# Moving the tensors of a two-block transformer kernel to other byte positions in SBUF

## The reference

```python
def first_block(...):                     # 2 layers; 512 latent + 256 context tokens
    for l in range(2):
        h = modulate(rms_norm(x, norm1_g[l]), sh1, sc1)
        qa, ka, va, qb, kb, vb, ga, gb = split_in_proj(h @ w_in[l])
        ya = window_attention_latent(...); yb = full_attention_latent(...)
        x = x + gt1 * ((sigmoid(ga) * (ya @ w_pa) + sigmoid(gb) * (yb @ w_pb)) @ w_o)
        h2 = modulate(rms_norm(x, norm2_g[l]), sh2, sc2)
        x = x + gt2 * ((silu(h2 @ w_gate) * (h2 @ w_up)) @ w_down)
        # in layer 0 the same is done for the context tokens
    return rms_norm(x, final_norm_g)

def second_block(x, ...):                 # 1 layer
    proj = rms_norm_2(x, norm_gain) @ w_in
    y_a = (nsa_mixer(...) * silu(g_nsa)) @ w_proj_a      # compressed, selected and windowed attention
    y_b = (rglru_mixer(u_lru, ...) * silu(g_lru)) @ w_proj_b
    return x + (sigmoid(gate_a) * y_a + sigmoid(gate_b) * y_b) @ w_out
```

## Time and profile before

| what | value |
|---|---|
| median of 3 runs | 2462.16 us |
| span of the profiled execution | 2459.3 us |
| mean granted TensorE clock | 0.992 of full |
| TensorE matmul busy | 2379.4 us, 97% |
| VectorE busy | 1547.7 us, 63% |
| ScalarE busy | 1129.1 us, 46% |
| chain that ended last | 79% TensorE |
| DMA, mean | 109 GB/s |

### The profile page before, as it was taken

The page is one execution under the profiler, slowest core; times in us unless marked ns, Lnnn a source line. Parts: engine busy times, 40 slices in busy tenths (PEclk is TensorE's granted clock), DMA queues, the critical chain, the costliest instruction groups (busy, mean ns, idle before and its releaser), DMA issues.

```text
span 2459.3 us, 32774 instructions
## 1 busy us (share of the span) xinstructions
PE 2379.4 (97%) x12351; PEld 1990.5 (81%) x12351; DVE 1547.7 (63%) x2398; ACT 1129.1 (46%) x1785; POOL 165.6 (7%) x292
## 2 busy tenths in 40 slices
PE   7999999999999999999999999999999999999898
PEld 3888877788888888888878877897888877877687
DVE  5786777788676554454686777754333367389763
ACT  5647777723321121122547777333222355467541
POOL 0200000110000000000100000100000010011020
PEclk9999999999999999999999999999999999999999
DMA  7421111363433333322221111522222334521263
GB/s 283 148 74 45 52 40 46 114 240 121 154 122 136 120 125 132 120 86 78 103 85 58 48 48 64 180 86 97 92 95 94 103 101 138 183 88 64 85 205 103
DMA packets 68866, 267.71 MB, mean 109 GB/s; under 512 B 8576, under 2 KB 8640, under 8 KB 67696
## 3 DMA queue, kind: packets, MB, share of 16 engines
q1 hardware_dynamic: 42336, 162.94, 19.2%
q0 software_dynamic: 26384, 102.77, 12.0%
HBM read 237.37 MB, written 27.26 MB: 108 GB/s over the span
## 4 chain that ended last, share of the span: by engine, by line
PE 79%; DVE 9%; ACT 6%; issue 4%; DMA 2%; POOL 0%; SPq 0%; ACTq 0%; DVEq 0%
PE ps L190 22%; PE ps L192 22%; PE ps L191 22%; DVE w_lo L186 2%; PE ps L1235 1%; PE ps L1236 1%; PE ps L1169 1%; PE ps L1237 1%; PE ps L1176 1%; DMA ada_raw<-in_ada 1%; DVE inv L1399 1%; ACT w_hi L179 1%; PE ps L1218 1%; ACT pr L1298 1%; DVE maxes L1422 1%
## 5 line engine op out<-in xcount | busy, mean ns | idle before, releaser
L190 PE MATMUL ps<-h_hi,w_hi 128*128 128x512 f32 (+2 forms) x2104 | 751.8, 357 | 14.4 <-DVE h_lo L1538 6.3
L192 PE MATMUL ps<-h_hi,w_lo 128*128 128x512 f32 (+2 forms) x2104 | 742.5, 353 | 0.0
L191 PE MATMUL ps<-h_lo,w_hi 128*128 128x512 f32 (+2 forms) x2104 | 741.6, 352 | 0.0
L186 DVE TENSOR_TENSOR w_lo<-w_raw,w_hi 128x1024 fp32r<-128x1024 f32 x288 | 358.3, 1245 | 199.7 <-ACT w_hi L179 199.5
L190 PEld LDWEIGHTS ps<-h_hi,w_hi 128*128 128x128 f32 x2104 | 398.0, 189 | 78.2 <-issue 14.3
L192 PEld LDWEIGHTS ps<-h_hi,w_lo 128*128 128x128 f32 x2104 | 398.4, 189 | 56.9
L191 PEld LDWEIGHTS ps<-h_lo,w_hi 128*128 128x128 f32 x2104 | 398.2, 189 | 56.4 <-issue 2.4
L179 ACT ACTIVATE w_hi<-w_raw 128x1024 fp32r<-128x1024 f32 x288 | 302.8, 1052 | 297.7 <-PE ps L192 288.1
L190 PE MATMUL ps<-q_hi,w_hi 128*128 128x512 f32 x720 | 256.1, 356 | 1.4 <-DVE q_lo L1559 1.4
L192 PE MATMUL ps<-q_hi,w_lo 128*128 128x512 f32 x720 | 256.7, 356 | 0.0
L191 PE MATMUL ps<-q_lo,w_hi 128*128 128x512 f32 x720 | 256.5, 356 | 0.0
(11 more groups left out here) (373 smaller groups left out, 3452.2 us busy)
## 6 DMA issues: line engine op xcount, KB each, us to landing
w_raw<-in_stream SPq DMA_DIRECT2D x288, 512.0 KB, 3.3
wt<-in_ada_t POOLq DMA_DIRECT2D x72, 512.0 KB, 3.6
ada_raw<-in_ada SPq DMA_DIRECT2D x4, 2048.0 KB, 18.0
x_keep<-x POOLq DMA_DIRECT2D x8, 768.0 KB, 7.8
gates<-th_g POOLq DMA_DIRECT2D x16, 384.0 KB, 2.6
gates<-sg POOLq DMA_DIRECT2D x24, 256.0 KB, 2.3
wt_q<-in_ada_t POOLq DMA_DIRECT2D x8, 512.0 KB, 3.6
gates<-th_g POOLq DMA_DIRECT2D x16, 256.0 KB, 2.3
```

Of the source, the lines that this page charges most:

```text
L186: nc.vector.tensor_tensor(w_lo[:, u % 3, :], raw[:, u % 2, :], w_hi[:, u % 3, :].bitcast(F32), ALU.subtract).then_inc(lo_ready, 1)
L190: nc.tensor.matmul(out_ap, lh, rh, start=start, stop=False)
L191: nc.tensor.matmul(out_ap, lh, rl, start=False, stop=False)
L192: return nc.tensor.matmul(out_ap, ll, rh, start=False, stop=stop)
```

## The change

The order in which SBUF tensors are declared changes. `region_h` moves from behind `region_x` to the end of the big regions, and the small tensors `aff`, `nsink`, `small`, `cs` and `cs4` move behind it. With that all big regions start 128 bytes past a multiple of 512 (table above). A row of `h` becomes 800 numbers (3200 bytes), so its eight chunks start at 128, 256, 384 and 0 past a multiple of 512, in turn. The region grows from 49280 to 51200 bytes. The scratch for dynamic DMAs is halved from 8192 to 4096 bytes.

`keep_awake` gets a list of operands. It issues the same numbers of matmuls at the same places, but their moving operand starts at other offsets in `w_hi` (0, 2, 16, 32, 48, 64, 96 or 128 numbers further), and some take `w_lo` as moving or as weight operand.

No instruction is added, removed or moved on any engine. Apart from addresses, only the tensors that 20 of these 64 matmuls name differ.

```diff
@@ constants
+H_ROW = 800
+AWAKE = {True: ([("hi", 16, "ident", 0), ("hi", 48, "ident", 0)], [("hi", 32, "ident", 0)], [("hi", 96, "ident", 0), ("hi", 2, "ident", 0)]),
+         False: ([("hi", 64, "ident", 0), ("hi", 128, "ident", 0)], [("lo", 0, "ident", 0)], [("hi", 48, "lo", 48), ("hi", 0, "lo", 48)])}
@@ build_program
         identR = sb("identR", [P, P], F32R)
-        aff = sb("aff", [P, DEPTH, 2, CH, 2])
-        nsink = sb("nsink", [P, 16])
-        small = sb("small", [P, 16])
-        cs = sb("cs", [P, 16])
-        cs4 = sb("cs4", [P, CH, 4], F32R)
-        gains = aff[:, 0, 0, :, 0]
         r_x = region("region_x", 4 * CH * TOK,
...
-        r_h = region("region_h", 8 * CH * (TOK + 2),
-                     [("h_hi", [P, CH, TOK + 2], F32R), ("h_lo", [P, CH, TOK + 2], F32R)],
...
@@ behind region_scratch
+        r_h = region("region_h", 8 * CH * H_ROW,
+                     [("h_hi", [P, CH, H_ROW], F32R), ("h_lo", [P, CH, H_ROW], F32R)],
...
+        aff = sb("aff", [P, DEPTH, 2, CH, 2])
+        nsink = sb("nsink", [P, 16])
+        small = sb("small", [P, 16])
+        cs = sb("cs", [P, 16])
+        cs4 = sb("cs4", [P, CH, 4], F32R)
+        gains = aff[:, 0, 0, :, 0]
@@ keep_awake
-        def keep_awake(u, count):
+        def keep_awake(u, count, *reads):
             for k in range(count):
-                nc.tensor.matmul(ps[:, 0, :], identR[:, :], w_hi[:, u % 3, 0:512], start=True, stop=True)
+                moving, m0, weights, w0 = reads[k * len(reads) // count]
+                tiles = {"hi": w_hi[:, u % 3, :], "lo": w_lo[:, u % 3, :], "ident": identR[:, :]}
+                nc.tensor.matmul(ps[:, 0, :], tiles[weights][:, w0:w0 + P], tiles[moving][:, m0:m0 + 512], start=True, stop=True)
@@ project
-                    keep_awake(base, 12)
+                    first, second_, third = AWAKE[stacked]
+                    keep_awake(base, 12, *first)
                     norm.statistic(e)
-                    keep_awake(base, 6)
+                    keep_awake(base, 6, *second_)
                     norm.spread(e)
-                    keep_awake(base, 14)
+                    keep_awake(base, 14, *third)
@@ kernel
-    nc = bacc.Bacc("TRN2", target_bir_lowering=False, num_devices=1, dynamic_dma_scratch_size=8192)
+    nc = bacc.Bacc("TRN2", target_bir_lowering=False, num_devices=1, dynamic_dma_scratch_size=4096)
```

More of the change, by code:

```diff
@@ L146, in build_program @@
                      [("ga", [P, 2, TOK], F32), ("gb", [P, 2, TOK], F32)], [("root_row", [P, TOK], F32), ("rooted_x", [P, 4, SEQ], F32)])
+        r_h = region("region_h", 8 * CH * H_ROW,
+                     [("h_hi", [P, CH, H_ROW], F32R), ("h_lo", [P, CH, H_ROW], F32R)],
+                     [("ada_raw", [P, 3, 4 * UNIT], F32)],
+                     [("h2_hi", [P, CH, SEQ], F32R), ("h2_lo", [P, CH, SEQ], F32R), ("r_hi", [P, 2, 16, 62], F32R),
+                      ("r_lo", [P, 2, 16, 62], F32R)],
+                     [("h2_below_s", [P, 2 * CH, SEQ], F32), ("s_hi", [P, 2, 4, SEQ], F32R)],
+                     [("h2_below_r", [P, 2 * CH, SEQ], F32), ("rg", [P, 4, SEQ], F32), ("ig", [P, 4, SEQ], F32)])
+        aff = sb("aff", [P, DEPTH, 2, CH, 2])
[4 more added lines that the diff above has]
+        gains = aff[:, 0, 0, :, 0]
         x, h_hi, h_lo = r_x["x"], r_h["h_hi"], r_h["h_lo"]
```

## The result

The changed kernel takes 2449.07 us, median of 4 runs (2446.04 to 2449.84); the kernel before, on the same chip, 2463.4 (2461.98 to 2466.8). The ratio is 0.9939, interval 0.9925 to 0.9953: 14.3 us faster. The forecast was 2432, 30 us faster. So the direction was right and about half of the gain did not come.

A forecast was written before the change was run, and what follows sets the result against it. The prediction took the rate at which TensorE's matmuls follow each other as the bound. Terms of 43.4 us, less 10.5 for half of `h`, gave 32.9; times 0.9, 30 us off 2462.16: 2432 us, 80% range 2408 to 2456.

The forecast's parts named there:

- the factor of 0.9: Whole kernel: a third of the gain lost in the attention stretches, a tenth overall, making 32.9 us into 30.
- attention, two terms: Attention matmuls: 640 gaining 6 ns each, 3.8 us, and some 700 narrower ones gaining 3 ns, 2.1 us.
- the two fast samples: `n_last` and `keep_awake`, 36 and 64 matmuls with operands at 128 past 512: both some 6 ns faster.
- The halving of `h`: `h` chunks at 128, 256, 384 and 0: half of their 21.1 us taken, between no gain and full gain.
- The narrow matmuls: `h` with 258 and 256 columns: 3 ns on 2400 matmuls, 7.2 us; `q` with 256: 1 ns, 0.7 us.
- Position makes no difference: Rival for all matmuls: the two samples are fast for another reason; 2462 us, chance 0.10.
- Only starts amid 16 bytes cost: Rival: only the four odd chunks of `h` in eight gain, 9.5 us; 2453 us, chance 0.05.
- Only 128 past 512 is good, and `h` gains nothing: Rival: operands other than `h` gain, 20 us in all; 2442 us, chance 0.20.
- Everything at `keep_awake`'s rate: Rival: all matmuls fall to its rate, 387 ns for 512 columns; 50 us faster, 2412 us, chance 0.17.
- The slower rival: Whole matmul stream: reads of moving operand and next weights meet, 398 ns; 30 us slower, 2492 us, chance 0.06.
- The rival in which half the scratch delays DMAs: Halved scratch delays GpSimd's DMAs so that columns of `wt` come late; 7.4 us to spare per load, chance 0.02.
- the tenth that was to be lost there: Attention stretches, 739 us of 2459: a third of their gain lost to waits for VectorE, a tenth of the whole.

The follow-up runs named there:

- e5: Changed kernel with only the weights moved, to 192 past a multiple of 512, activations staying at 128: 2459.49 us, ratio 0.9985.
- p1: Changed kernel with a long list of `keep_awake` matmuls at the second block's start, 16 per kind, probing offsets and widths; its 2575.87 us is not of interest.
- e1: Changed kernel with rows of `h` of 832 numbers (3328 bytes) instead of 800: 2441.88 us, ratio 0.9914.
- e8: Changed kernel with rows of `h` of 770 numbers and the DMA scratch back at 8192 bytes: 2450.54 us, ratio 0.9945.
- e4: Changed kernel with weights and activations alike 64 bytes further, at 192 past a multiple of 512: 2450.81 us, ratio 0.9941.
- e12: Changed kernel, `h` rows of 832, context tokens 192 bytes further when feeding the projection, 64 when feeding layer 0's FFN: 2441.19 us, ratio 0.9909.
- e10: Changed kernel, `h` rows of 832 numbers with 64 bytes left free between latent and context tokens: 2442.3 us, ratio 0.9918.

## Why the prediction was half right

The bound was read rightly: the kernel is bound by the distance of matmuls. But the change also acts elsewhere: 3.0 us of the gain are the shorter DRAIN, and the second `keep_awake` lost 2.1. The sign, the interval and the size for the operands that run alone held. By terms (forecast before the factor of 0.9, then measured from the starts):

```
term                            forecast us    measured us
n                                   -5.0          -5.3
y                                   -1.2          -1.2
h2                                  -2.3          -2.3
q, 512 columns                      -7.2          -4.7 (layer 1), +0.5 (layer 0)
q, 256 columns                      -0.7          +1.0
h, 512 columns                      -7.0 (half)   -1.9
h, 256 and 258 columns              -3.6 (half)    about 0
attention, two terms                -5.9           about 0
sum                                 -32.9         -13.9
DRAIN at the end (scratch)           0            -3.0
second keep_awake (clock)            0            +2.1
```

The spans differ by 11.4 us and the medians by 14.3. The 3.4 us left between the rows of this table and the spans are small waits, mostly in the attention, and where the other stretches of the low clock fall. The value of `h2` was measured on 265 of its 376 triples and scaled up.

**The step that failed** is the one that reads the two fast samples: "I take 389 ns as the aligned price of 512 columns", for every operand at a multiple of 128 bytes, with counts taken over all matmuls of a width. The samples were good, 389 is what `n`, `y` and `h2` reached. What failed is carrying it over to the rest: the terms, priced at 32.9 us, measured 13.9. Both samples had two more things in common than the place. Weights and moving operand lay at *equal* places modulo 256; e5 took just that away and 389 became 394 to 396. And `keep_awake` stood in a run of its own width; layer 0's `q` has the same positions and keeps 5.5 ns.

**The halving of `h`** stood for not knowing whether only chunk places at 128 count. In fact a mixture of distance 0 and 128, chunk by chunk, is worth almost nothing (5.4 to 5.1 ns), not half. The low distance needs several matmuls in a row to settle (p1). The whole gain was one number away: e1.

**The narrow matmuls** were priced at half of the wide ones' gain, on the grounds that no aligned one stood in the trace. The bound on the loss side was missing. At distance 0 they are slow (120 ns in p1, where 64 gives 113.3), and `q` with 256 columns, at 278 before, had been fast *because* it lay 192 bytes off (320 less 128): e5, 192 bytes off again with the activations at 128, brings the 278 back. The row stood there: 278 for `q_lo` against 282 for `h_lo`. It was read as the floor of an aligned matmul when it was the profit of an unaligned one.

**The scratch** was counted at nothing, with a few microseconds of loss as the bound, because only the loads of `wt` were looked at. It gave 3.0 us at the end of the program (e8), where no load is issued at all. So a fifth to a quarter of the whole gain came from a term that stands at zero in the forecast, and in so far the time came nearer to the forecast by luck. **`keep_awake`** was bounded by 9 ns per matmul, under 0.6 us. The one of the second block took 2.1 us longer, nearly all of it in the stretch of the low clock.

**Attention** did not move: `p_lo` stands at 395 as before. Which neighbour or width keeps it there was not tried.

**The rivals.** "Position makes no difference" is refuted by e5. "Only starts amid 16 bytes cost" is refuted by `n` and `q`, which were on whole lines and gained most. "Only 128 past 512 is good, and `h` gains nothing" had the right consequence for `h` and came closest in time (2442), for a wrong reason: e4 has nothing at 128 past 512 and is as fast as after. "Everything at `keep_awake`'s rate" was true of the lonely operands: they reached 227 ns. The slower rival, equal positions that collide, is true of 256 columns alone. The rival in which half the scratch delays DMAs is refuted with the sign turned round: it saved 3.0 us (e8).

**The stated signs.** `keep_awake`'s new operands were to tell whether a multiple of 128 counts. The median of line 494 is 394, for offsets of 64, 128 and 192 bytes alike about 233 ns from start to start; 256 bytes further it is 227 at once. So 256 is the period, and that could be read from the trace of after before any experiment. The gaps of the attention stretches were to grow and did not; the tenth that was to be lost there can't be told apart from their missing gain.

## What to carry to other kernels

Where a stream of matmuls bounds the kernel, compare the byte positions of moving operand and weights with each other, modulo 256, instead of rounding each to something even, and price each width on its own: here 512 columns want distance 0 in long runs of one width, 256 columns want 64 or 192. Make the pitch of a tensor whose slices are moving operands a multiple of that period. When a small sample in a trace is fast, list everything in which it differs from the rest (its weights, its neighbours, the length of the run) before it is counted up to all the rest, and bound the unknown widths on the loss side too. When a part of a change is counted at nothing, compare the last microseconds of the two traces, behind the last matmul, before you credit the whole difference to the rest.

## What the runs showed of the hardware

- The lowest steady distance of float32r matmuls here is 226.7 ns for 512 columns and 113.3 for 256: at 2.4 GHz 544 and 272 cycles, 17 for every 16 columns. No position tried went below it. The Trainium skill (page "TensorE: Matmul & The Clock Gate", section "Back-to-back issue gap") gives N / 2.4 plus 2.5 ns as the gap of single matmuls at the full clock, which is 215.8 for 512 columns, and about 131 ns for a sustained stream of them with its weight loads. No stream in these traces reached either.
- Other distances cost up to 7 ns at 512 columns and up to 7 at 256, and the pattern repeats over a few matmuls (233, 236, 228, ...). In p1 even equal places needed about nine matmuls after a change of both to settle at 226.7. Why was not found; a meeting of the reads of weights and moving operand fits e5, but no run isolates it.
- A standstill of 2.6 us in 10 in a busy stretch (7.45 busy in e12) went with a fall of the granted clock to 0.91 behind it; 2.0 us (7.98 busy in e10, not shown) and 1.7 us (8.28 busy in after) did not. An order that makes TensorE wait a little longer can thus cost more than the wait.
- GpSimd's DRAIN at the end of the program takes 4.07 us with 8192 bytes of scratch for dynamic DMAs and 1.05 us with 4096, the same to the nanosecond in every profile. Other sizes were not tried.
